# One hybrid decoder layer: the first norm folded into the modulation rows, its output rows made later, memsets, two loads and first loop counts moved

## The reference, cut to what matters

```python
mix = jnp.concatenate([attn, conv], axis=-1) @ w_o
x = layer_norm(DEEPNORM_ALPHA * x + (1 + gate1) * mix, ln1_g, ln1_b)
u2 = x * (1 + scale2) + shift2
ffn = moe(u2, router_w, router_b, w_up, b_up, w_down, b_down)
x = layer_norm(DEEPNORM_ALPHA * x + (1 + gate2) * ffn, ln2_g, ln2_b)
```

## Time and profile before

| | us |
|---|---|
| median of 3 runs | 1505.88 (1501.29 to 1507.79) |
| profiled execution, its own time | 1502.87 |
| its span, first to last instruction | 1501.1 |
| PE busy | 1415.1 (94% of the span) |
| DVE busy | 499.0 (33%) |
| ACT busy | 244.7 (16%) |
| POOL busy | 13.7 (1%) |
| DMA moved | 523.72 MB, 349 GB/s over the span |

### The profile page before, as it was taken

One profiled execution on the slowest core, in us unless ns is written; L12 is line 12 of the kernel. 1 busy time (PEld: TensorE's weight loads), 2 busy tenths in 40 slices (PEclk: granted clock), 3 DMA queues, 4 the chain that ended last, 5 costly groups with the idle time before them and its releaser, 6 DMA issues.

```text
span 1501.1 us, 22079 instructions
## 1 busy us (share of the span) xinstructions
PE 1415.1 (94%) x7645; PEld 578.4 (39%) x7646; DVE 499.0 (33%) x1127; ACT 244.7 (16%) x431; POOL 13.7 (1%) x22
## 2 busy tenths in 40 slices
PE   5999999999949999999999999999999999999993
PEld 2654666665533333333333323333333333333331
DVE  2210355554671223232323232323222332313336
ACT  0001334442020111111111111111111111101110
POOL 0000000000010000000000000000000000000000
PEclk9999999999969999999999999999999999999997
DMA  9948456999857789999999988999999999998941
GB/s 337 391 167 315 176 185 266 419 424 386 251 192 278 284 352 401 418 418 418 415 418 417 419 352 359 406 418 418 417 416 419 417 418 416 418 401 322 385 191 35
DMA packets 95716, 523.72 MB, mean 349 GB/s; under 512 B 10172, under 2 KB 10485, under 8 KB 55498
## 3 DMA queue, kind: packets, MB, share of 16 engines
q1 hardware_dynamic: 92512, 517.62, 86.1%
q0 software_dynamic: 1344, 4.90, 0.8%
q10 hardware_dynamic: 1834, 0.84, 0.3%
HBM read 519.87 MB, written 3.46 MB: 349 GB/s over the span
## 4 chain that ended last, share of the span: by engine, by line
PE 83%; DMA 8%; DVE 5%; SPq 2%; issue 2%; ACT 0%; DVEq 0%
PE ps L1635 28%; PE ps L1713 14%; PE ps L1578 7%; PE ps L1192 6%; PE ps L1252 5%; PE ps L1556 5%; DMA arena<-in_cache_v 4%; PE ps L1480 3%; DMA arena<-in_w_in 2%; PE ps L1627 2%; PE ps L1249 2%; PE ps L1422 2%; DMA arena<-in_w_up 2%; PE ps L1645 1%; PE ps L1405 1%
## 5 line engine op out<-in xcount | busy, mean ns | idle before, releaser
L1635 PE MATMUL ps<-arena 128*64 128x512 f32 x2048 | 451.9, 599 | 0.6 <-DMA arena<-in_w_up 0.6
L1635 PEld LDWEIGHTS ps<-arena 128*64 128x64 f32 x2048 | 144.7, 138 | 306.7 <-issue 304.2
L1713 PE MATMUL ps<-arena 128*64 128x512 f32 x1024 | 226.8, 595 | 0.0
L1094 DVE TENSOR_TENSOR arena<-arena,ps 128x512 f32<-128x512 f32 (+1 forms) x198 | 124.4, 680 | 220.6 <-PE ps L1578 214.9
L1192 PE MATMUL ps<-arena 128*128 128x128 f32 (+4 forms) x1075 | 151.6, 282 | 33.6 <-DVEq L975 10.9
L1138 DVE TENSOR_SCALAR arena<-ps 128x512 f32<-128x512 f32 (+1 forms) x35 | 24.2, 692 | 419.7 <-PE ps L1635 358.6
L1192 PEld LDWEIGHTS ps<-arena 128*128 128x128 f32 (+4 forms) x1075 | 116.8, 144 | 107.9 <-issue 80.3
L1713 PEld LDWEIGHTS ps<-arena 128*64 128x64 f32 x1024 | 70.7, 137 | 152.2 <-issue 152.2
L1578 PE MATMUL ps<-arena 64*128 64x512 f32 x444 | 122.1, 635 | 4.9 <-DVE arena L1118 4.6
L1556 PE MATMUL ps<-arena 128*64 128x512 f32 (+1 forms) x396 | 97.1, 608 | 2.3 <-DVE arena L1082 2.3
L670 ACT ACTIVATE arena<-arena 128x512 f32<-128x512 f32 (+1 forms) x35 | 22.1, 632 | 447.8 <-DVE arena L1138 447.8
(11 more groups left out here) (225 smaller groups left out, 839.7 us busy)
## 6 DMA issues: line engine op xcount, KB each, us to landing
arena<-in_w_up SPq DMA_DIRECT2D x256, 1024.0 KB, 14.4
arena<-in_w_down SPq DMA_DIRECT2D x128, 1024.0 KB, 12.4
arena<-in_w_ada SPq DMA_DIRECT2D x12, 2048.0 KB, 17.8
arena<-in_cache_k SPq DMA_DIRECT2D x16, 1536.0 KB, 14.3
arena<-in_cache_v SPq DMA_DIRECT2D x16, 1536.0 KB, 9.7
arena<-in_w_in SPq DMA_DIRECT2D x6, 2048.0 KB, 20.5
arena<-in_cache_k SPq DMA_DIRECT2D x32, 192.0 KB, 12.9
arena<-in_cache_v SPq DMA_DIRECT2D x32, 192.0 KB, 10.9
```

The source lines that it names most:

```text
L1094: ins = v_.tensor_tensor(acc[0:n, tt, 512 * h:512 * h + 512], acc[0:n, tt, 512 * h:512 * h + 512], bank(banks[h])[0:n], ALU.add)
L1635: ins = mm(bank(part)[64 * h:64 * h + 64], xe_t[:, 0, at:at + 64], up_w[:, k, FF * part + 512 * h:FF * part + 512 * h + 512], start=False, ...
L1713: ins = mm(bank(3)[64 * h:64 * h + 64], a_t[:, 0, at:at + 64], dn_w[:, kk, 512 * h:512 * h + 512], start=kk == 0, stop=kk == KC - 1)
```

## The change

The products of the first norm's vectors with the modulation vectors are made once for each of `mod_p` and `mod_s` (`fold_norm`): with s = 1 + scale2, the shift row becomes shift2 + s * ln1_b and the scale row becomes s * ln1_g. Then u2 is made from the raw rows in two instructions, (x - mean) * scale row and * (1 / deviation) + shift row. The normed x, still needed at the end, is made by `keep_rows`: tile 0 right after its u2, tiles 1 and 2 after `route_ready`. Mean and reciprocal deviation are kept for each tile (columns 50 and on of `st`).

`fold_norm(mod_p)` stands in the last batch on DVE, between `mask_output` and `keep_output` of batch 6; `fold_norm(mod_s)` after that batch, ahead of `residual_sums(0)`. `ln1_b` goes to a place inside the down weights, so the first down weights' load waits until `keep_rows` is done (`x1_kept`). `head_mask` moves, and `mod_s` is loaded right after `mod_p`. The rows of tile 2 are loaded later, the memsets of POOL move, the four gate instructions of `route` become one, and two of PE's and ACT's steps ahead of the expert loop change place.

```diff
             sp.wait_ge(og_ready, 1)
-            for a, name in enumerate(("ln1_g", "ln1_b")):
-                sp.dma_start(ln1[a], t[name][0:1, :].to_broadcast([128, D])).then_inc(tail_in, 16)
+            sp.dma_start(ln1[0], t["ln1_g"][0:1, :].to_broadcast([128, D])).then_inc(tail_in, 16)
             sp.wait_ge(vec_out, 64)
             sp.wait_ge(s_done, NB)
+            sp.dma_start(ln1[1], t["ln1_b"][0:1, :].to_broadcast([128, D])).then_inc(tail_in, 16)
             sp.dma_start(mod_p, vectors[0:1, 0:3 * D].to_broadcast([128, 3 * D]).rearrange("p (a b) -> p a b", a=3)
                          ).then_inc(mod_in, 16)
+            for b in range(NB):
+                src = vectors[1 + b:2 + b, 0:3 * D].to_broadcast([NS, 3 * D]).rearrange("p (a b) -> p a b", a=3)
+                sp.dma_start(mod_s[NS * b:NS * b + NS], src).then_inc(mod_late, 16)
             sp.wait_ge(s_max, NB + 1)
             sp.dma_start(x1[:, 0, :], t["x_prompt"][0, 0:128, :]).then_inc(tail_in, 16)
             load_values(slice(NB - 1, NB), NB - 1)
             sp.wait_ge(st_done, 3 * NB)
             sp.dma_start(x1[:, 1, :], t["x_prompt"][0, 128:256, :]).then_inc(x_late, 16)
-            sp.dma_start(x1[0:64, 2, :], t["x_sample"].rearrange("b s d -> (b s) d")).then_inc(x_late, 16)
...
             sp.wait_ge(so_copied, NB)
-            for b in range(NB):
-                src = vectors[1 + b:2 + b, 0:3 * D].to_broadcast([NS, 3 * D]).rearrange("p (a b) -> p a b", a=3)
-                sp.dma_start(mod_s[NS * b:NS * b + NS], src).then_inc(mod_late, 16)
+            sp.dma_start(x1[0:64, 2, :], t["x_sample"].rearrange("b s d -> (b s) d")).then_inc(x_late, 16)
             for k in range(4, KC):
                 sp.dma_start(up_w[:, k, :], wup_d[0, k]).then_inc(up_in[k], 16)
-            for m in range(KC // 2):
-                if m == 1:
-                    sp.wait_ge(u2_ready, 3)
+            sp.wait_ge(u2_ready, 3)
+            for m in (1, 2, 3, 0):
+                if m == 0:
+                    sp.wait_ge(x1_kept, 1)
                 sp.dma_start(dn_w[:, 2 * m:2 * m + 2, :], wdn_d[0, m]).then_inc(dn_in[m], 16)
             sp.wait_ge(route_ready, 1)
             load_expert(0, None)
...
+            pool.wait_ge(og_ready, 2)
+            nc.gpsimd.memset(y_sb, 0.0)
+            nc.gpsimd.memset(sel_t, 0.0).then_inc(cleared, 1)
             pool.wait_ge(wo_done, 3)
+            pool.dma_start(bd_sb[0:NE, :], t["b_down"][0]).then_inc(late_in, 16)
+            pool.wait_ge(sel_ready, 1)
             nc.gpsimd.memset(acc, 0.0).then_inc(acc_ready, 1)
-            pool.dma_start(bd_sb[0:NE, :], t["b_down"][0]).then_inc(late_in, 16)
-            nc.gpsimd.memset(y_sb, 0.0)
-            pool.wait_ge(u2_ready, 3)
-            nc.gpsimd.memset(sel_t, 0.0).then_inc(cleared, 1)
+            pool.wait_ge(x1_kept, 1)
             for a, name in enumerate(("ln2_g", "ln2_b")):
                 pool.dma_start(ln2[a], t[name][0:1, :].to_broadcast([128, D])).then_inc(ln2_in, 16)
...
+            def fold_norm(mod, n):
+                part = mix[0:n, 1, :]
+                V(v_.scalar_tensor_tensor(part, mod[0:n, 2, :], 1.0, ln1[1][0:n, :], ALU.add, ALU.mult))
+                V(v_.tensor_tensor(mod[0:n, 1, :], mod[0:n, 1, :], part, ALU.add))
+                V(v_.scalar_tensor_tensor(mod[0:n, 2, :], mod[0:n, 2, :], 1.0, ln1[0][0:n, :], ALU.add, ALU.mult))
 
             def residual_norm(tt):
-                n = TILES[tt][1]
+                n, mv = TILES[tt][1], 50 + 4 * tt
+                mod = mod_p if tt < 2 else mod_s
+                dve.wait_ge(sd_ready, (2, 4, 5)[tt])
+                V(v_.reciprocal(st[0:n, mv + 2:mv + 3], st[0:n, 36:37]))
+                V(v_.scalar_tensor_tensor(mix[0:n, tt % 2, :], x1[0:n, tt, :], st[0:n, mv:mv + 1], mod[0:n, 2, :],
+                                          ALU.subtract, ALU.mult))
+
+            def modulate(tt):
+                V(v_.scalar_tensor_tensor(u2[0:n, tt, :], mix[0:n, tt % 2, :], st[0:n, mv + 2:mv + 3], mod[0:n, 1, :],
+                                          ALU.mult, ALU.add))
+                dve.sem_inc(u2_ready, 1)
+
+            def keep_rows(tt):
                 x_t = x1[0:n, tt, :]
-                norm_rows(dve, V, v_, x_t, n, st, ln1, sd_ready, (2, 4, 5)[tt], x_t)
-
-            def modulate(tt):
-                V(v_.scalar_tensor_tensor(u2[0:n, tt, :], mod[0:n, 2, :], 1.0, x_t, ALU.add, ALU.mult))
-                V(v_.tensor_tensor(u2[0:n, tt, :], u2[0:n, tt, :], mod[0:n, 1, :], ALU.add))
-                dve.sem_inc(u2_ready, 1)
+                V(v_.scalar_tensor_tensor(x_t, x_t, st[0:n, mv:mv + 1], ln1[0][0:n, :], ALU.subtract, ALU.mult))
+                V(v_.scalar_tensor_tensor(x_t, x_t, st[0:n, mv + 2:mv + 3], ln1[1][0:n, :], ALU.mult, ALU.add))
...
                 if more:
                     dve_turned(0, b + 1)
+                else:
+                    dve.wait_ge(mod_in, 16)
+                    dve.wait_ge(tail_in, 48)
+                    fold_norm(mod_p, 128)
                 if not first:
                     keep_output(b - 1)
...
             dve_batch(NB - 1, False, False)
+            dve.wait_ge(mod_late, 128)
+            fold_norm(mod_s, 64)
             residual_sums(0)
             residual_norm(0)
             mask_output(NB - 1)
+            modulate(0)
+            keep_rows(0)
             keep_output(NB - 1)
...
             squares(1)
-            modulate(0)
             mean_squares(1)
...
-                for r in range(ROUNDS):
-                    v_.tensor_scalar(gate_t[0:n, tt, NE * r:NE * r + NE], ex[0:n, :], st[0:n, 41:42], None, ALU.mult)
-                V(v_.memset(gate_t[0:n, tt, ITEMS:ITEMS + 1], 0.0))
+                V(v_.tensor_scalar(gate_t[0:n, tt, 0:ITEMS].rearrange("p (r e) -> p r e", r=ROUNDS),
+                                   ex[0:n, :].unsqueeze(1).to_broadcast([n, ROUNDS, NE]), st[0:n, 41:42], None, ALU.mult))
...
+            keep_rows(1)
+            keep_rows(2)
+            dve.sem_inc(x1_kept, 1)
 
             gathered_turned(2, 1)
             dve.wait_ge(acc_ready, 1)
...
             turn_gathered(2, 1)
             turn_gates()
-            pe.wait_ge(gt_ready, 1)
             with pe.Fori(0, items) as i:
```

More of the change, by code:

```diff
@@ L124, in layer_kernel @@
         kt_sb = view(KTX, AC, NCACHE)
[L125 to L128, removed]
+        assert KTX + AC * NCACHE <= 24576
         P = 24576
@@ L174, in layer_kernel @@
         prob = view(R1 + SB, NCACHE + 64)
+        head_mask = view(R1 + SB + NCACHE + 64, 256)
+        query_sum = view(R1 + SB + NCACHE + 320, 3, 8)
         x1 = view(R1, 3, D)
@@ L215, in layer_kernel @@
         u2_t = view(R4 + 3 * D, KC, 128)
-        ln1 = [view(R5, D), view(R2 + 2 * D, D)]
+        ln1 = [view(R5, D), view(W + 16 * D, D)]
         xe_t = view(R4, 2, 512)
@@ L279, in layer_kernel @@
             sem, ("u2_ready", "u2t_done", "u2t_ready", "lg_done", "neg_ready", "ex_ready", "masks_ready"))
-        rank_done, route_ready, gt_done, gt_ready, acc_ready, late_in, ln2_in, cleared = map(
-            sem, ("rank_done", "route_ready", "gt_done", "gt_ready", "acc_ready", "late_in", "ln2_in", "cleared"))
+        rank_done, route_ready, gt_done, gt_ready, acc_ready, late_in, ln2_in, cleared, x1_kept = map(
+            sem, ("rank_done", "route_ready", "gt_done", "gt_ready", "acc_ready", "late_in", "ln2_in", "cleared", "x1_kept"))
         sel_ready, selg_ready, y_ready = sem("sel_ready"), sem("selg_ready"), sem("y_ready")
@@ L647, in _ @@
             act.wait_ge(route_ready, 1)
-            for counted_from_one in (y_ready, selt_ready):
-                act.sem_inc(counted_from_one, 1)
             items = act.value_load(flag_i[0:1, 0:1], min_val=NE, max_val=ITEMS)
@@ L662, in _ @@
             nc.scalar.copy(gt_sb[0:NE, :], bank(6, 0, NTOK)[0:NE]).then_inc(gt_ready, 1)
+            act.wait_ge(gt_ready, 1)
+            for counted_from_one in (y_ready, selt_ready):
+                act.sem_inc(counted_from_one, 1)
             with act.Fori(0, items) as i:
@@ L960, in residual_sums @@
                 V(v_.scalar_tensor_tensor(x_t, x_t, ALPHA, m, ALU.mult, ALU.add))
-                norm_sums(V, v_, x_t, n, st, var_ready)
-            def residual_norm(tt):
-                n = TILES[tt][1]
-                x_t = x1[0:n, tt, :]
-                norm_rows(dve, V, v_, x_t, n, st, ln1, sd_ready, (2, 4, 5)[tt], x_t)
-            def modulate(tt):
-                n = TILES[tt][1]
-                x_t, mod = x1[0:n, tt, :], mod_p if tt < 2 else mod_s
-                V(v_.scalar_tensor_tensor(u2[0:n, tt, :], mod[0:n, 2, :], 1.0, x_t, ALU.add, ALU.mult))
-                V(v_.tensor_tensor(u2[0:n, tt, :], u2[0:n, tt, :], mod[0:n, 1, :], ALU.add))
-                dve.sem_inc(u2_ready, 1)
+                norm_sums(V, v_, x_t, n, st, 50 + 4 * tt, var_ready)
+            def fold_norm(mod, n):
[3 more added lines that the diff above has]
```

(21 more changed lines are left out.)

2 lines of the change are left out of this document (1 added, 1 removed).

## The result

| | before | after |
|---|---|---|
| time, median of 5 runs, us | 1501.29 (1500.89 to 1507.79) | 1515.74 (1510.17 to 1517.34) |
| profiled execution, own time, us | 1502.87 | 1510.17 |
| its span, us | 1501.1 | 1508.4 |
| its mean granted TensorE clock | 0.975 | 0.974 |

The ratio is 1.0073 [1.0053, 1.0093]: the change makes the kernel some 11 us slower (the two medians alone differ by 14.4, but single runs spread by 7). The forecast of 1515.9 us, slower, was right.

The account below looks back on a forecast made before the run. PE bounds nearly everything, except a dip at 412 to 450 us set by DVE's chain. PE idle +12.1, clock +1.4 and dip gain -3.5 make +10.0 us on the 1505.88 median: 1515.9 us, own range 1511 to 1521.

Parts of the forecast that it names:

- The transfers, 10 us: SP's queue ahead of x1: eight mod_s transfers take 10 us (ends 1.9 and 12), so x1's tile 0 lands at 380.9.
- PE idle, 12.1 us: Last batch: fold_norm(mod_p) waits for x1 ahead of batch 6's output copy, so PE's transposes start at 385.2, not 373.06.
- The clock, 1.4 us: After PE's long pause in the last batch, its clock stays at half speed for 2.9 us, costing 1.4 us.
- the sum: Whole kernel: +12.1 PE idle, +1.4 clock, -3.5 dip gain, together +10.0 us.
- The values of batch 7, hidden: Last batch: values land at 391 at the latest, PE needs them at 394.6, so their delay hides behind the stall.
- The gain in the dip, 3.5 us: Router stretch ahead of the expert loop: DVE's shorter chain starts the first expert 3.5 us earlier (ends 1.5 and 8.1).
- The flag chain blocked: In the dip: POOL's moved acc memset blocks DVE's flag chain until 433.7; unblocked it would be done 2.2 us earlier.
- `y_sb` and `sel_t` at no cost: Their memsets beside DVE's tile 1 instructions cost nothing; if they did block, at most 2.65 us.
- Rival 1: mod_s transfers cost only their bytes: PE stalls 4.0 to 5.8 us, total +1 to +4, 1508.5 us; chance 0.20.
- Rival 2: x1 passes the eight loads, bias rows come early: PE loses 2.0, dip gives 8.1, total -6, 1500 us; chance 0.12.
- Rival 3: Dip's gain misses the expert loop: x1_kept, down weights, bias rows land at 450 or later, 1519.4 us; chance 0.06.
- From the profile to the median: Profiled 1502.87 us was 3 us under the median of 1505.88; the difference was put on that median, giving 1515.9 us.

Follow-up runs that it names:

- e3: Changed kernel with the wait for route_ready and the first expert's bias rows ahead of the x1_kept wait and last down weights; ratio to before 1.0045.
- e5: Changed kernel with only POOL's acc memset waiting for route_ready instead of sel_ready (the first choice); ratio to before 1.0051.
- e2: Changed kernel with the eight mod_s transfers moved behind batch 7's values and fold_norm(mod_s) behind squares(1); ratio to before 0.9996.
- e1: Changed kernel with fold_norm(mod_p) moved from ahead of batch 6's keep_output to behind the last batch, loads unmoved; ratio to before 1.0034.
- e6: Kernel before with only SP's new order: eight mod_s transfers behind mod_p, x_sample loaded later, head_mask and query_sum moved; ratio to before 1.0079.
- e4: Changed kernel, mod_s transfers behind batch 7's values, both folds behind PE's copies, bias rows before last down weights, acc memset behind route_ready; ratio to before 0.9954.
- e11: As e4, but the mod_s transfers issued only when batch 7's values have landed, ahead of the first up weights; ratio to before 0.9963.

## Why the prediction was right

Point by point, with its own steps:

- **The transfers, 10 us, and what stands behind them: right in kind, 2 us too large in the profiled execution.** The step put x1's tile 0 at 20.6 us behind the value product (380.9 in the times of before), 10 later than before's 10.6. The fold began at 18.5 in after, and at 20.5 and 20.3 in e3 and e5: 7.9, 9.8 and 9.7 us late. (Against e2, as in the table, it is 10.1 to 12.1.) From issue to landing it took 15.3 us in after and 18.3 and 17.8 in e3 and e5, where 18 was named. In e2, with the eight elsewhere, DVE's wait is 2.76 us instead of 12.90, which shows the cause.
- **PE idle, 12.1 us: measured 9.8**, and 11.7 and 11.6 in e3 and e5, which have the same order. The term is right in kind and 2.3 too large in the profiled execution, 0.4 to 0.5 in the others; nearly all of it is x1's landing.
- **The clock, 1.4 us: too small.** The transposes and `output(0, 1)` took 2.4 us more, and 1.7 to 3.1 in the other executions with this stall: the clock read 0.50 up to 384 and 0.79 from 384 to 385, some 5 us into PE's work, where the step had taken the 2.9 us of the gather. Not foreseen was that it fell again later, while PE was fully busy (windows of after):

```profile
414.00:415.00 1.00, 1.00 (x10) 0.92 (x11) 0.97 (x3) 0.00 (x0) 0.00 (x0) 1.00 0.99 410
415.00:416.00 1.00, 1.00 (x4) 0.27 (x4) 0.66 (x4) 0.60 (x2) 0.00 (x0) 0.57 1.06 442
...
417.00:418.00 1.00, 1.00 (x4) 0.24 (x2) 0.96 (x2) 0.00 (x0) 0.00 (x0) 0.50 0.40 164
418.00:419.00 1.00, 1.00 (x6) 0.39 (x4) 0.81 (x3) 0.00 (x0) 0.00 (x0) 0.72 0.06 25
```

  That made `output_sample` 8.79 us instead of 7.09. The gather took 5.02 instead of 4.42, which is hidden in PE's wait for the bias rows. Stall and clock together come to 9.8 + 2.4 + 1.7 = 13.9 ahead of the dip's part, where the sum had 13.5: wrong sizes that cancel, which is luck.
- **The values of batch 7, hidden: right here, by luck of a larger wait.** In after the last of them was issued at 364.0 and none took more than 20.4 us to land, and PE came for them at 389.75. But the step took it for granted that they cost something only as far as they stand behind the eight. e1, e2 and e6 show that they are the second limit, with 9.5 us of their own (2.05 even where the eight follow them). The prediction didn't say that a kernel without the fold's stall would be slow as well; e6 is.
- **The gain in the dip, 3.5 us: measured 3.55.** Its parts: tile 2's residual starts 4.7 us earlier against the end of `output_sample` (0.21 instead of 4.88), as worked out. The choice comes 7.6 us earlier in that frame, as worked out. The flag chain behind which `route_ready` stands ends 4.0 us after the choice's end (4.5), `keep_rows` takes 5.24 us (5.3), and from there to the bias product it is 6.4 (6.2).
- **The flag chain blocked: right**, with 2.23 us for four tiny instructions that take 0.43 unblocked (e5). The `tensor_reduce` and the memset of one row ahead of them, both beside POOL's memset too, were not blocked (0.17 each, as in e5); the blocked form is the `tensor_scalar`.
- **`y_sb` and `sel_t` at no cost: right.** L951 and L963 beside them take 1.22 and 1.23 us.
- **The rivals.** Rival 1 (only the bytes) falls by x1's delay of 8 us or more and by PE's 9.8 us, where it had 4.0 to 5.8. Rival 2 (x1 passes the eight, early bias rows) falls by the fold's 375.25, which is 378.8 in the times of before, and by the 6.96 us. Rival 3 (the dip's gain lost) falls by the 3.55.
- **From the profile to the median: luck.** The sum was put on a median of 1505.88 us of three runs; that of five runs is 1501.29, 4.6 lower, and 10.0 on that would be 1511.3. That 1515.9 and 1515.74 agree so closely is chance: what the runs support is the ratio, 8 to 14 us. Single falls of the clock, told below, are one source of such scatter.

## What to carry to other kernels

A transfer that is moved earlier in a queue is priced by what stands behind it, up to the last load that an engine waits for: eight small transfers of 0.79 MB in all held up the next load by 8 to 12 us and the kernel by 11, and each experiment that freed one waiter found the next behind it. When a fused or shorter chain ends earlier, look for the queue that was never late before; here it was two waits of SP in the wrong order (4.3 us) and a memset beside one-row flags (2.1). And put work that has to wait for a transfer behind the small copy for which TensorE waits, not ahead of it.

## What the runs showed of the hardware that was not expected

**The clock also falls while PE is busy.** In most of the expert loop one expert takes 29.4 us from its neighbour's start to its own, and there the granted clock read 0.99 or more throughout. A few experts take 32 to 46 us, and beside those it falls now and then; a line is then 1.7 us longer. The same expert in e4 and in before:

```profile
486.86 8.78 PE L1664 MATMUL ps<-arena 128*64 128x512 f32 x32
```

```profile
490.37 7.09 PE L1635 MATMUL ps<-arena 128*64 128x512 f32 x32
```

In e4 the granted clock read 0.74 from 487 to 488, 0.50 up to 490 and 0.55 from 490 to 491, with PE busy in all of each; the last pause of PE of more than 1 us ended at 473. Behind the first expert there are two such falls in before (at 533 and 1373 us) and in after (541, 1381), and three in e4 (487, 862, 1371). Each lasts some 3 us and costs 1.7. Beside which of the long experts they come differs between executions of kernels that are the same there, so they are one source of the spread of single times, and a difference of 2 or 3 us between two profiled executions shows nothing by itself. Why the clock falls there, the rows don't tell.

**A queue's slow transfers also hold up what was issued ahead of them.** In e2 and e4 the eight follow batch 7's values, and PE waits 2.05 and 4.55 us for the values all the same, where it waited for nothing before. It is the slowest of the four small values that is late, with 15.5 and 18.0 us from issue to landing, instead of 13.5 in before and 12.9 in e11, where the eight are issued only when the values have landed; the medians are as before (10.7 and 12.1 us, instead of 11.8). x1's tile 1, issued behind the eight, took 14.6 and 16.7 us instead of 6.9. The rows show it, and no run here tells why.
